# Attention by pairs of heads with one transpose bank and shared copies, and expert tokens transposed four experts at a time

## The chip, the cores and the metric

One core of a Trainium2 chip runs the whole program. The metric is device time in microseconds (us), the median of several executions. Beside it there is one profiled execution, from which all rows below come.

## The reference

One inference step of a two-layer backbone on 256 context tokens and 1024 latent tokens, width 1024, all in fp32. Layer 0 mixes by a long convolution and by attention (8 query heads of 64, 2 key heads); layer 1 by a gated linear recurrence. Each layer ends with 16 experts, each of which picks its own tokens: 32 of the context and 128 of the latents. What the change touches, cut to its core:

```python
def block_attention(q, k, v):                    # per head and block of 128 queries
    s = jnp.einsum('bqkgd,bskd->bkgqs', qblk, k) * scale
    p = jax.nn.softmax(s, axis=-1)
    return jnp.einsum('bkgqs,bskd->bqkgd', p, v)

def expert_choice_ffn(h, router_w, w_gu, w_down):
    aff = softmax(xf @ router_w); gate, idx = lax.top_k(aff.T, cap)
    xin = xf[idx]
    a, u = jnp.split(jnp.einsum('ecd,edf->ecf', xin, w_gu), 2, axis=-1)
    out = jnp.einsum('ecf,efd->ecd', jax.nn.silu(a) * u, w_down) * gate[..., None]
    return zeros.at[idx.reshape(-1)].add(out.reshape(-1, D))
```

Context queries see the 256 context keys (2 tiles of 128), latent queries the cached context and all latents (10 tiles).

## The kernel before

The program is a chain of stages, each a block of five instruction streams (PE, ACT, DVE, POOL, SP) that wait for one another by semaphores; a stream's order is its order in the code.

**Attention** (`attention`, line 900) goes through 80 items, each one head and one tile of 128 queries: 64 latent items with 10 key tiles and 16 context items with 2. Of an item, PE computes the scores (call them S, line 930: 512, 512 and 256 columns, contraction over the 64 rows of one head), DVE takes the row maximum (lines 996, 998), ACT the exponential with its row sum (972), DVE normalises (1000 to 1002), PE transposes the probabilities (T, line 957: 10 tiles of 128x128), ACT copies them from PSUM to SBUF (984) and PE multiplies by the values (P, line 941, 64 output rows); DVE copies the result out (1008). The scores have one buffer of three PSUM banks, the transposes four banks `t_ps`, the output one. PE's order is S of item i+1, T of item i, P of item i-1. The two heads of a pair stand in rows 0 to 63 and 64 to 127 of `qT` and `kT`, and their results in the same halves of `o_ps`.

**Experts** (`experts`, line 1283, once per layer, after `route`, line 1152): SP streams 12 MB of weights per expert in 12 pieces. POOL gathers the 128 latent and the 32 context rows of the next expert (lines 1338, 1339) and scatters the results. PE transposes the gathered rows (lines 1370, 1371) into one PSUM tile of 2x160 columns, in four groups of two latent and two context transposes each; ACT scales them into `xT` (1431). Then PE computes 16 chains of 8 matmuls on 160 columns (gate and up, line 1385), ACT and DVE form silu(a) times u (1439, 1461), and PE multiplies by the down weights, for latents (1398) and, as four column groups of 32, for context (1408). The groups of transposes for expert e+1 stand after the gate and up matmuls of e and between its four down chains. Experts 0 to 14 run as a hardware loop on every engine.

Of the kernel before, what the change touches and what calls it, by code (L numbers as in the profile page):

```python
# [899 lines left out]
def attention(nc, A, S, qT, kT, v, yT):  # L900


    items = [(2 * pr + r, t, 0 if t < CT else CT, CT if t < CT else KT - CT)
             for pr in range(4) for t in range(NT) for r in range(2)]
    N = len(items)
    chunks = [[(k, min(4, nk - k)) for k in range(0, nk, 4)] for _, _, _, nk in items]
    first = [sum(len(c) for c in chunks[:i]) for i in range(N + 1)]
    KMAX = KT - CT
    with ExitStack() as ctx:
        sb, ps, sem = scope(nc, ctx, "att")  # L910
        p = sb("p", [P, 2, KMAX * P])
        pT = sb("pT", [P, 2, KMAX, P])
        top, part = sb("top", [P, N, 3]), sb("part", [P, N, 3])
        nmax, total = sb("nmax", [P, N]), sb("total", [P, N])
# [3 lines left out]
        qk, maxed, exped, normed, v_steps, tr, tr_out, pv, o_out = (  # L918
            sem("qk"), sem("maxed"), sem("exped"), sem("normed"), sem("v"), sem("tr"), sem("tr_out"), sem("pv"), sem("o_out"))
        block = ctx.enter_context(nc.Block())  # L920

        @block.tensor
        def _(pe):
            def scores(i):
                h, t, k0, nk = items[i]
                r = h % 2
                for j, (k, n) in enumerate(chunks[i]):
                    if i >= 1:
                        pe.wait_ge(exped, min(first[i - 1] + j + 1, first[i]))
                    nc.tensor.matmul(s_ps[:, k * P:(k + n) * P], qT[64 * r:64 * r + HD, h // 2, t * P:(t + 1) * P],  # L930
                                     kT[64 * r:64 * r + HD, h // 4, (k0 + k) * P:(k0 + k + n) * P], start=True, stop=True).then_inc(qk, 1)

            def products(i):
                h, t, k0, nk = items[i]
                r = h % 2
                if i >= 2:
                    pe.wait_ge(o_out, i - 1)
                for j, (k, n) in enumerate(chunks[i]):
                    pe.wait_ge(tr_out, first[i] + j + 1)
                    for a in range(k, k + n):  # L940
                        m = nc.tensor.matmul(o_ps[64 * r:64 * r + HD, 0:P], v[:, k0 + a, (h // 4) * HD:(h // 4 + 1) * HD],  # L941
                                             pT[:, i % 2, a, :], start=(a == 0), stop=(a == nk - 1))
                m.then_inc(pv, 1)

            scores(0)
            for i in range(N):
                h, t, k0, nk = items[i]
                r = h % 2
                if i + 1 < N:
                    scores(i + 1)  # L950
                pe.wait_ge(normed, i + 1)
                for j, (k, n) in enumerate(chunks[i]):
                    c = first[i] + j
                    if c >= 4:
                        pe.wait_ge(tr_out, c - 3)
                    for a in range(n):
                        m = nc.tensor.transpose(t_ps[c % 4][:, a * P:(a + 1) * P], p[:, i % 2, (k + a) * P:(k + a + 1) * P],
                                                S["ident"][:, :])
                    m.then_inc(tr, 1)
                if i >= 1:  # L960
                    products(i - 1)
            products(N - 1)

        @block.scalar
        def _(act):
            def exps(i):
                h, t, k0, nk = items[i]
                act.wait_ge(maxed, i + 1)
                if i >= 2:
                    act.wait_ge(tr, first[i - 1])  # L970
                for j, (k, n) in enumerate(chunks[i]):
                    nc.scalar.activation(p[:, i % 2, k * P:(k + n) * P], s_ps[:, k * P:(k + n) * P], ACT.Exp, bias=nmax[:, i:i + 1],  # L972
                                         accum_out=part[:, i, j:j + 1]).then_inc(exped, 1)

            exps(0)
            for i in range(N):
                if i + 1 < N:
                    exps(i + 1)
                if i >= 2:
                    act.wait_ge(pv, i - 1)  # L980
                for j, (k, n) in enumerate(chunks[i]):
                    c = first[i] + j
                    act.wait_ge(tr, c + 1)
                    nc.scalar.activation(pT[:, i % 2, k:k + n, :].rearrange("p a c -> p (a c)"), t_ps[c % 4][:, 0:n * P],
                                         ACT.Copy).then_inc(tr_out, 1)

        @block.vector
        def _(dve):
            steps = Count(v_steps)

            def softmax(i):
                h, t, k0, nk = items[i]
                nch = len(chunks[i])
                for j, (k, n) in enumerate(chunks[i]):
                    dve.wait_ge(qk, first[i] + j + 1)
                    r = nc.vector.tensor_reduce(top[:, i, j:j + 1], s_ps[:, k * P:(k + n) * P], AX_X, ALU.max)
                steps.link(dve, r)
                nc.vector.tensor_reduce(nmax[:, i:i + 1], top[:, i, 0:nch], AX_X, ALU.max, negate=True).then_inc(maxed, 1)  # L998
                dve.wait_ge(exped, first[i + 1])
                steps.link(dve, nc.vector.reduce_sum(total[:, i:i + 1], part[:, i, 0:nch], AX_X))  # L1000
                steps.link(dve, nc.vector.reciprocal(total[:, i:i + 1], total[:, i:i + 1]))
                nc.vector.tensor_scalar(p[:, i % 2, 0:nk * P], p[:, i % 2, 0:nk * P], total[:, i:i + 1], None, ALU.mult).then_inc(normed, 1)

            def output(i):
                h, t, _, _ = items[i]
                r = h % 2
                dve.wait_ge(pv, i + 1)
                nc.vector.tensor_copy(yT[64 * r:64 * r + HD, h // 2, t * P:(t + 1) * P], o_ps[64 * r:64 * r + HD, 0:P]).then_inc(o_out, 1)

            softmax(0)  # L1010
            for i in range(N):
                if i + 1 < N:
                    softmax(i + 1)
                if i >= 1:
                    output(i - 1)
            output(N - 1)
# [124 lines left out]
def load_expert(sp, A, layer, w, w_in, j, e):  # L1141

    if j < 8:
        jj, part = divmod(j, 2)
        c0 = part * FH + jj * SW
        src = A["moe_w_gu"][layer][bass.ds(e, 1), :, c0:c0 + SW]
    else:
        src = A["moe_w_down"][layer][bass.ds(e, 1), :, (j - 8) * SW:(j - 7) * SW]
    sp.dma_start(w[:, j, :, :], src.rearrange("a (k p) n -> p (a k) n", p=P)).then_inc(w_in[j], 16)


def route(nc, A, S, tag, hnT, layer, idx, gates, expert_w, expert_w_in, next_modulation=False):
# [3 lines left out]
    with ExitStack() as ctx:  # L1156
# [12 lines left out]
        pt = ps("pt", [P, 4 * NE])  # L1169
# [21 lines left out]
        def _(pe):  # L1191
# [41 lines left out]
        def _(dve):  # L1233
# [37 lines left out]
            dve.wait_ge(tr2, 1)  # L1271
            for c in range(2):
# [10 lines left out]
def experts(nc, A, S, tag, layer, xn_dram, x_dram, idx, gates, w, w_in):  # L1283
# [6 lines left out]
    CC = CP + CL  # L1290
    with ExitStack() as ctx:
        sb, ps, sem = scope(nc, ctx, tag)
        xl, xc = sb("xl", [P, D]), sb("xc", [CP, D])
        xT = sb("xT", [P, KD, CC])
# [3 lines left out]
        icg, ics = [sb("icg0", [CP, 1], U32), sb("icg1", [P, 1], U32)], [sb("ics0", [CP, 1], U32), sb("ics1", [P, 1], U32)]  # L1298
        gate_f = sb("gate_f", [P, 2, D])
        pgu = [ps(f"pgu{i}", [P, CC]) for i in range(4)]  # L1300
        pxt = ps("pxt", [P, 2 * CC])
# [5 lines left out]
        gate_in, p_steps, o_free, issued = sem("gate_in"), sem("p_steps"), sem("o_free"), sem("issued")  # L1307
        block = ctx.enter_context(nc.Block())

        @block.sync  # L1310
        def _(sp):
# [7 lines left out]
            with sp.Fori(1, NE) as e:  # L1319
                for j in range(12):  # L1320
                    if j < 8 and j % 2 == 0:
                        sp.wait_ge(gu_mm, e * 16 + (4 * (j // 2) + 4 - 16))
# [889 lines left out]
```

## Time and profile before

| | us |
|---|---|
| median of 3 runs (4649.28 to 4650.81) | 4650.71 |
| the profiled execution | 4647.39 |
| its span, first to last instruction | 4645.6 |
| PE busy in the span | 4148.2 (89%) |
| DVE, ACT, POOL busy | 1825.1, 1245.0, 200.7 |
| mean granted TensorE clock | 0.945 of 2.4 GHz |

PE = TensorE matmul, PEld = its weight loads (which overlap), DVE = VectorE, ACT = ScalarE, POOL = GpSimd, SP = SyncE. Attention takes the stretch from 651 to 1078 us, the experts of layer 0 that from 1345 to about 2270, those of layer 1 that up to 4606. An fp32 matmul shows in the records as two passes. A matmul's recorded end is modelled, so the start of the next block is the better mark.

### The profile page before, as it was taken

Reading aid. Unit: us, or ns where it says so; the run is one execution under the profiler, and the core shown is the slowest. Engines: PE = TensorE matmul, PEld = TensorE weight load, DVE = VectorE, ACT = ScalarE, POOL = GpSimd, SP = SyncE. Lnnn points to the kernel's source line nnn. Section 1 sums busy time; section 2 is a strip of 40 time slices with the busy share of each in tenths; the row PEclk is TensorE's granted clock in tenths of the full one; section 3 lists DMA queues with packets and bytes.
Section 4 is the critical chain, followed back from the end, with each engine's and each line's share of the span. In section 5 each row is a group of like instructions: output and inputs, shape, how many; then the busy total and the mean of one; then the engine's idle time right before and its main releaser. Section 6 shows DMA issues by size and latency. Waiting matters only on the chain. (4 is left out here: it accounts for less than half of the span.)

```text
span 4645.6 us, 59698 instructions
## 1 busy us (share of the span) xinstructions
PE 4148.2 (89%) x23973; PEld 3289.7 (71%) x23973; DVE 1825.1 (39%) x3112; ACT 1245.0 (27%) x2593; POOL 200.7 (4%) x304
## 2 busy tenths in 40 slices
PE   5798999999759999999699999999768299999996
PEld 1454456665339999998588888888644199999995
DVE  4324355552351111111248888888832611111111
ACT  1211135552201111111244454444423011111111
POOL 0000000000000000001000000000000001000000
PEclk8899989999879999999799999999889599999998
DMA  6201100003487888777410101110032478888884
GB/s 224 86 14 58 35 1 1 1 1 118 174 273 244 252 249 248 239 239 239 123 29 26 31 16 31 31 31 17 7 137 95 129 224 252 251 252 251 251 249 160
DMA packets 522238, 614.81 MB, mean 132 GB/s; under 512 B 16460, under 2 KB 466632, under 8 KB 521449
## 3 DMA queue, kind: packets, MB, share of 16 engines
q1 hardware_dynamic: 502216, 543.33, 36.0%
q0 software_dynamic: 16832, 58.73, 5.0%
q10 hardware_dynamic: 3040, 10.68, 0.6%
q8 instruction: 102, 1.67, 0.1%
q14 instruction: 48, 0.39, 0.0%
HBM read 558.86 MB, written 53.84 MB: 132 GB/s over the span
## 5 line engine op out<-in xcount | busy, mean ns | idle before, releaser
L1385 PEld LDWEIGHTS moe_pgu<-moe_xT,mw_w 128*128 128x128 f32 x8192 | 1118.7, 191 | 15.6 <-issue 15.6
L1385 PE MATMUL moe_pgu<-moe_xT,mw_w 128*128 128x160 f32 x8192 | 1126.4, 300 | 3.0 <-ACT moe_xT L1431 3.0
L1461 DVE TENSOR_TENSOR moe_hT<-moe_sg,moe_pgu 128x160 f32<-128x160 f32 x256 | 82.3, 322 | 1028.0 <-PE moe_pgu L1385 944.9
L1398 PE MATMUL moe_pol<-mw_w,moe_hT 128*128 128x256 f32 x2048 | 474.6, 385 | 0.8 <-DVE moe_hT L1461 0.8
L1642 PE MATMUL rec_pz<-step_hnT,rec_w 128*128 128x256 f32 x1920 | 425.1, 380 | 10.8 <-DMA rec_w<-in_r_w_in 8.8
L1398 PEld LDWEIGHTS moe_pol<-mw_w,moe_hT 128*128 128x128 f32 x2048 | 379.0, 190 | 52.8 <-DVE moe_hT L1461 1.3
L1642 PEld LDWEIGHTS rec_pz<-step_hnT,rec_w 128*128 128x128 f32 x1920 | 362.8, 191 | 59.7 <-DMA rec_w<-in_r_w_in 9.1
L1439 ACT ACTIVATE moe_sg<-moe_pgu 128x160 f32<-128x160 f32 x256 | 77.8, 304 | 1124.9 <-PE moe_pgu L1385 1124.9
L1431 ACT ACTIVATE moe_xT<-moe_pxt,step_modcol 128x128 f32<-128x128 f32 (+1 forms) x512 | 172.5, 417 | 534.2 <-PE moe_pxt L1371 534.2
L1646 PE MATMUL rec_pz<-rec_w,step_hnT 128*128 128x256 f32 x1280 | 284.8, 381 | 15.2 <-ACT rec_zg L1717 15.2
L1646 PEld LDWEIGHTS rec_pz<-rec_w,step_hnT 128*128 128x128 f32 x1280 | 241.5, 191 | 49.8 <-ACT rec_zg L1717 18.0
L1465 DVE SCALAR_TENSOR_TENSOR moe_ol<-moe_pol,step_gates,moe_gate_f 128x512 f32<-128x512 f32 x64 | 48.1, 751 | 518.6 <-PE moe_pol L1398 518.6
L1672 PE MATMUL rec_pg<-rec_ring 128*128 128x128 f32 x1600 | 198.3, 283 | 49.9 <-DVE rec_AT L1958 18.6
L1672 PEld LDWEIGHTS rec_pg<-rec_ring 128*128 128x128 f32 x1600 | 194.6, 198 | 55.6 <-DVE rec_ring L1937 20.3
L383 PE MATMUL hin_psm<-step_hnT,hin_w 128*128 128x512 f32 (+1 forms) x576 | 209.1, 526 | 10.6 <-DMA hin_w<-in_e_w_in 10.6
L383 PEld LDWEIGHTS hin_psm<-step_hnT,hin_w 128*128 128x128 f32 x576 | 110.7, 193 | 106.3 <-issue 89.9
L930 PE MATMUL att_s_ps<-l0p_kT,l0p_qT 64*128 64x512 f32 (+1 forms) x416 | 172.2, 545 | 10.4 <-ACT att_p L972 8.6
L972 ACT ACTIVATE att_p<-att_s_ps,att_nmax 128x512 f32<-128x512 f32 (+1 forms) x208 | 123.7, 602 | 205.7 <-DVE att_nmax L998 205.7
L941 PE MATMUL att_o_ps<-att_pT,l0p_v 128*64 128x128 f32 x1344 | 165.6, 278 | 0.0
L1085 PE MATMUL op_psm<-op_w,l1o_yr 128*128 128x512 f32 x320 | 142.8, 603 | 19.2 <-DMA l1o_yr<-scratch_yr 19.2
L941 PEld LDWEIGHTS att_o_ps<-att_pT,l0p_v 128*64 128x64 f32 x1344 | 145.9, 138 | 14.0 <-issue 13.4
L1770 ACT ACTIVATE rec_ring<-rec_ring 128x1280 f32<-128x1280 f32 x112 | 138.5, 1264 | 37.2 <-DVE rec_ring L1914 32.3
(316 smaller groups left out, 4648.7 us busy)
## 6 DMA issues: line engine op xcount, KB each, us to landing
mw_w<-in_moe_w_gu SPq DMA_DIRECT2D x256, 1024.0 KB, 10.1
mw_w<-in_moe_w_down SPq DMA_DIRECT2D x128, 1024.0 KB, 10.2
mod_w_ring<-in_mod_w SPq DMA_DIRECT2D x24, 1024.0 KB, 14.4
mw_w<-in_mod_w SPq DMA_DIRECT2D x24, 1024.0 KB, 14.3
rec_w<-in_r_w_in SPq DMA_DIRECT2D x40, 512.0 KB, 3.9
scratch_xm<-op_x ACTq DMA_DIRECT2D x20, 512.0 KB, 2.6
scratch_xn<-op_xn POOLq DMA_DIRECT2D x20, 512.0 KB, 5.1
hin_w<-in_e_w_in SPq DMA_DIRECT2D x12, 512.0 KB, 6.7
```

The costliest lines, as they stand in the source:

```text
L383: m = nc.tensor.matmul(psm[j % NPS][:, 0:n * P], w[:, i % 2, k, part, :], hnT[:, k, t0 * P:(t0 + n) * P], start=(k == 0), stop=(k == KD - 1))
L930: nc.tensor.matmul(s_ps[:, k * P:(k + n) * P], qT[64 * r:64 * r + HD, h // 2, t * P:(t + 1) * P], kT[64 * r:64 * r + HD, h // 4, (k0 + k) ...
L941: m = nc.tensor.matmul(o_ps[64 * r:64 * r + HD, 0:P], v[:, k0 + a, (h // 4) * HD:(h // 4 + 1) * HD], pT[:, i % 2, a, :], start=(a == 0), s ...
L972: nc.scalar.activation(p[:, i % 2, k * P:(k + n) * P], s_ps[:, k * P:(k + n) * P], ACT.Exp, bias=nmax[:, i:i + 1], accum_out=part[:, i, j: ...
L1085: m = nc.tensor.matmul(psm[t % NB][:, h * 512:(h + 1) * 512], lhs(k)[:, t * P:(t + 1) * P], w[:, k, h * 512:(h + 1) * 512], start=(k == 0) ...
L1385: m = nc.tensor.matmul(pgu[2 * (f % 2) + part][:, :], w[:, j, k, (f % 2) * P:(f % 2 + 1) * P], xT[:, k, :], start=(k == 0), stop=(k == KD ...
L1398: m = nc.tensor.matmul(pol[q // 2][:, (q % 2) * SW:(q % 2 + 1) * SW], hT[:, k, 0:CL], w[:, 8 + q, k, :], start=(k == 0), stop=(k == KD - 1))
L1431: r = nc.scalar.activation(xT[:, k, c0:c0 + n], pxt[:, j * CC + c0:j * CC + c0 + n], ACT.Identity, bias=mc[:, layer, 3, c, k:k + 1], scale ...
L1642: m = nc.tensor.matmul(pz[i % 3][:, 0:2 * P], w[:, k, n // NZU, :], hnT[:, k, c0:c0 + 2 * P], start=(k == 0), stop=(k == KD - 1))
L1646: m = nc.tensor.matmul(pz[i % 3][:, 0:2 * RD], hnT[:, k, t * P:(t + 1) * P], w[:, k, 3:5, :].rearrange("p a c -> p (a c)"), start=(k == 0) ...
L1672: into_banks(h, (d, i), lambda o, t: nc.tensor.matmul(o, kb[:, t * P:(t + 1) * P], qb[:, t * P:(t + 1) * P], start=True, stop=True))
L1770: nc.scalar.activation(r, r, ACT.Exp).then_inc(exped, 1)
```

## The change

Attention: an item is now a pair of heads, 40 pairs in all, the 8 context pairs first. The scores have two buffers of three banks, one per head; S alternates between the two heads' row halves, P between their output halves. The probabilities are transposed in groups of four tiles into one single bank; ACT copies groups 0, 1, 2 and 4 of a latent pair and DVE group 3. Maximum and exponential take up to 1024 and 1280 columns in one instruction. PE's order is T group 0, S of the next pair, then T groups 1 to 4 with a slice of the P of the pair before after each.

Experts: the context rows of four experts are gathered and transposed together (128 rows), into a ring in `hnT`; a context turn stands after experts 3, 7 and 11. A turn is two groups of four 128x128 transposes. `route` gains four small matmuls and a copy that form the index `idx_four`. The hardware loops are unrolled, POOL's index copies are gone, and the scatter's wait stands before the next scatter.

```diff
-    items = [(2 * pr + r, t, 0 if t < CT else CT, CT if t < CT else KT - CT)
-             for pr in range(4) for t in range(NT) for r in range(2)]
+    pairs = [(pr, t, 0, CT) for pr in range(4) for t in range(CT)] + [(pr, t, CT, KT - CT) for pr in range(4) for t in range(CT, NT)]
+    groups = [[tl[g:g + 4] for g in range(0, len(tl), 4)] for tl in tiles]
+    by_dve = [g == 3 for gr in groups for g in range(len(gr))]
...
-        s_ps = ps("s_ps", [P, 3 * 512])
-        t_ps = [ps(f"t_ps{i}", [P, 512]) for i in range(4)]
+        s_ps = ps("s_ps", [P, 2, 3 * 512])
+        t_ps = ps("t_ps", [P, 512])
...
+            def scores(i, j):
+                for r in range(2):
+                    if i:
+                        pe.wait_ge(exped, 2 * (i - 1) + r + 1)
+                    nc.tensor.matmul(s_ps[:, r, k * P:(k + n) * P], qT[64 * r:64 * r + HD, pr, t * P:(t + 1) * P],
...
+            def transposes(i, g):
+                pe.wait_ge(normed, 2 * i + 1 + max(r for r, _ in group))
+                copied(pe, gfirst[i] + g)
...
+            def products(i, a0, a1):
+                if a0 == 0:
+                    copied(pe, gfirst[i + 1])
+                    if i:
+                        pe.wait_ge(o_out, i)
+                for a in range(a0, a1):
+                    for r in range(2):
...
+                for g in range(ng):
+                    transposes(i, g)
+                    if g == 0 and i + 1 < N:
+                        for j in range(len(chunks[i + 1])):
+                            scores(i + 1, j)
+                    if i and (g or ng == 1):
...
+                for g in range(3):
+                    copy(i, g)
+                if i + 1 < N:
+                    exp(i + 1, 0)
+                copy(i, 4)
+                if i + 1 < N:
+                    exp(i + 1, 1)
...
+                if i + 1 < N:
+                    maxes(i + 1)
+                copy(i, 3)
+                if i + 1 < N:
+                    normalise(i + 1, 0)
+                if i + 1 < N:
+                    normalise(i + 1, 1)
+                if i:
+                    output(i - 1)
...
+            for j in range(4):
+                m = nc.tensor.matmul(pt[32 * j:32 * j + CAP[0], 4 * NE:], topf[:, 0, 0:CAP[0]], S["ident"][0:NE, j:NE:4],
+                                     start=True, stop=True, tile_position=(0, 32 * j))
...
+        turns = [("c", 0), ("l", 0)]
+        for e in range(1, NE):
+            turns += [("l", e)] + ([("c", e // 4)] if e % 4 == 0 else [])
...
+                for j in range(4):
+                    m = nc.tensor.transpose(pxt[:, j * P:(j + 1) * P], src[:, (4 * g + j) * P:(4 * g + j + 1) * P], S["ident"][:, :])
...
+                moves = [(turn, g) for turn in coming(e) for g in range(2)]
+                if moves:
+                    transposes(*moves[0])
+                pe.wait_ge(multiplied, NF * (e + 1))
...
+                    if q + 1 < len(moves):
+                        transposes(*moves[q + 1])
```

PE in the middle of attention before, one latent item: S (L930) of the next item, T (L957) of this one into three of the four banks `att_t_ps0` to `att_t_ps3`, P (L941) of the one before.

```order
L930 MATMUL att_s_ps<-l0p_kT,l0p_qT 128x512 x2
L930 MATMUL att_s_ps<-l0p_kT,l0p_qT 128x256
L957 MATMUL att_t_ps3<-step_ident,att_p 128x128 x4
L957 MATMUL att_t_ps0<-step_ident,att_p 128x128 x4
L957 MATMUL att_t_ps1<-step_ident,att_p 128x128 x2
L941 MATMUL att_o_ps<-att_pT,l0p_v 64x128 x10
```

PE at the same place now, one latent pair (S is L942, T is L951, P is L962), from S to the group of transposes that begins the next pair:

```order
L942 MATMUL att_s_ps<-l0p_kT,l0p_qT 128x512 x4
L942 MATMUL att_s_ps<-l0p_kT,l0p_qT 128x256 x2
L951 MATMUL att_t_ps<-step_ident,att_p 128x128 x4
L962 MATMUL att_o_ps<-att_pT,l0p_v 64x128 x4
L951 MATMUL att_t_ps<-step_ident,att_p 128x128 x4
L962 MATMUL att_o_ps<-att_pT,l0p_v 64x128 x6
L951 MATMUL att_t_ps<-step_ident,att_p 128x128 x4
L962 MATMUL att_o_ps<-att_pT,l0p_v 64x128 x4
L951 MATMUL att_t_ps<-step_ident,att_p 128x128 x4
L962 MATMUL att_o_ps<-att_pT,l0p_v 64x128 x6
L951 MATMUL att_t_ps<-step_ident,att_p 128x128 x4
```

Two heads share one S block and one P block cut in four, and every group of T goes into the same bank.

ACT in the middle of attention before: the three exponentials (L972) of the next item, then the three copies (L984) of this one.

```order
L972 ACTIVATE att_p,att_part<-att_s_ps,att_nmax 128x512 x2
L972 ACTIVATE att_p,att_part<-att_s_ps,att_nmax 128x256
L984 ACTIVATE att_pT<-att_t_ps3 128x512
L984 ACTIVATE att_pT<-att_t_ps0 128x512
L984 ACTIVATE att_pT<-att_t_ps1 128x256
```

ACT there now: the second head's exponential (L991) of one pair, copies of groups 0 to 2 (L999), the next pair's first exponential, the copy of group 4, and its second exponential.

```order
L991 ACTIVATE att_p,att_total<-att_s_ps,att_nmax 128x1280
L999 ACTIVATE att_pT<-att_t_ps 128x512 x3
L991 ACTIVATE att_p,att_total<-att_s_ps,att_nmax 128x1280
L999 ACTIVATE att_pT<-att_t_ps 128x512
L991 ACTIVATE att_p,att_total<-att_s_ps,att_nmax 128x1280
```

The second exponential stands behind the copy of the last group, and the next pair's first copy behind that exponential.

PE at the end of the gate and up matmuls of an expert before (`moe_xl` are latent rows, `moe_xc` context rows; the rows without a tile are the loop's registers and waits):

```order
L1385 MATMUL moe_pgu<-moe_xT,mw_w 128x160 x16
L1389 REGISTER_ALU
L1370 MATMUL moe_pxt<-step_ident,moe_xl 128x128
L1371 MATMUL moe_pxt<-step_ident,moe_xc 128x32
L1370 MATMUL moe_pxt<-step_ident,moe_xl 128x128
L1371 MATMUL moe_pxt<-step_ident,moe_xc 128x32
L1392 REGISTER_ALU
L1396 ISA
L1398 MATMUL moe_pol<-mw_w,moe_hT 128x256 x8
L1403 REGISTER_ALU
L1370 MATMUL moe_pxt<-step_ident,moe_xl 128x128
L1371 MATMUL moe_pxt<-step_ident,moe_xc 128x32
```

PE there now, a whole expert without a context turn:

```order
L1455 MATMUL moe_pgu<-step_hnT,mw_w 128x160 x128
L1438 MATMUL moe_pxt<-step_ident,moe_xl 128x128 x4
L1467 MATMUL moe_pol<-mw_w,moe_hT 128x256 x8
L1438 MATMUL moe_pxt<-step_ident,moe_xl 128x128 x4
L1467 MATMUL moe_pol<-mw_w,moe_hT 128x256 x24
L1477 MATMUL moe_poc<-mw_w,moe_hT 32x256 x32
```

Two groups of four stand where four groups of four stood; after experts 3, 7 and 11 there are four.

## Rows read from the trace of the kernel before

**Rows 1.** Waits in attention, 650 to 1075: engine, line, releaser: us, times, longest

```profile
ACT att_p L972 <- DVE att_nmax L998: 205.7, 80, 5.4
```

**Rows 2.** Timeline of PE in attention: start, us, engine, line, operation

```profile
804.94 2.41 PE L930 MATMUL att_s_ps<-l0p_kT,l0p_qT 64*128 64x512 f32 x6
807.28 1.31 PE L957 MATMUL att_t_ps<-step_ident,att_p 128*128 128x128 f32 x10
808.52 2.40 PE L941 MATMUL att_o_ps<-att_pT,l0p_v 128*64 128x128 f32 x20
810.85 2.41 PE L930 MATMUL att_s_ps<-l0p_kT,l0p_qT 64*128 64x512 f32 x6
```

**Rows 3.** Groups by line and shape in attention: busy us, mean ns | idle before

```profile
L996 DVE TENSOR_REDUCE att_top<-att_s_ps 128x1 f32<-128x512 f32 x128 | 87.6, 690 | 29.3 <-PE att_s_ps L930 28.8
L972 ACT ACTIVATE att_p<-att_s_ps,att_nmax 128x512 f32<-128x512 f32 x128 | 86.9, 683 | 178.5 <-DVE att_nmax L998 178.5
L984 ACT ACTIVATE att_pT<-att_t_ps 128x512 f32<-128x512 f32 x128 | 69.7, 606 | 0.9 <-PE att_t_ps L957 0.9
L1002 DVE TENSOR_SCALAR att_p<-att_p,att_total 128x1280 f32<-128x1280 f32 x64 | 56.7, 886 | 2.2
L972 ACT ACTIVATE att_p<-att_s_ps,att_nmax 128x256 f32<-128x256 f32 x80 | 37.8, 473 | 27.2 <-DVE att_nmax L998 27.2
L996 DVE TENSOR_REDUCE att_top<-att_s_ps 128x1 f32<-128x256 f32 x80 | 33.3, 416 | 8.7 <-PE att_s_ps L930 8.6
```

**Rows 4.** Timeline of the expert stage, PE, one whole expert

```profile
1422.27 35.04 PE L1385 MATMUL moe_pgu<-moe_xT,mw_w 128*128 128x160 f32 x256
1457.15 0.27 PE L1370 MATMUL moe_pxt<-step_ident,moe_xl 128*128 128x128 f32 x1
...
1457.96 3.72 PE L1398 MATMUL moe_pol<-mw_w,moe_hT 128*128 128x256 f32 x16
...
1474.71 3.66 PE L1408 MATMUL moe_poc<-mw_w,moe_hT 128*32 128x256 f32 x64
1478.30 5.97 PE L1385 MATMUL moe_pgu<-moe_xT,mw_w 128*128 128x160 f32 x42
```

**Rows 5.** Timeline of the last item of attention, all engines

```profile
1072.09 1.31 PE L957 MATMUL att_t_ps<-step_ident,att_p 128*128 128x128 f32 x10 [0.55 <-DVE att_p L1002]
1072.85 1.36 ACT L984 ACTIVATE att_pT<-att_t_ps 128x512 f32<-128x512 f32 x3 [0.87 <-PE att_t_ps L957]
...
1073.34 4.20 PE L941 MATMUL att_o_ps<-att_pT,l0p_v 128*64 128x128 f32 x40
...
1077.57 0.29 DVE L1008 COPY l_filt<-att_o_ps 64x128 f32<-64x128 f32 x1 [1.52 <-PE att_o_ps L941]
```

**Rows 6.** Timeline of the first context items of attention

```profile
651.01 1.19 PE L930 MATMUL att_s_ps<-l0p_kT,l0p_qT 64*128 64x256 f32 x2 [1.76 <-PEq L80]
...
653.26 0.19 ACT L972 ACTIVATION_READ_ACCUMULATOR att_p<-att_s_ps,att_nmax 128x1 f32 x1
```

**Rows 7.** Windows: us, busy by engine, granted clock, DMA share, GB/s

```profile
651.00:661.00 10.00, 8.00 (x20) 3.95 (x21) 4.52 (x18) 3.76 (x10) 0.00 (x0) 0.50 0.00 1
771.00:781.00 10.00, 8.41 (x36) 4.43 (x35) 5.57 (x16) 4.40 (x14) 0.00 (x0) 1.00 0.00 0
1480.20:1538.60 58.40, 58.40 (x419) 53.10 (x419) 6.27 (x15) 9.40 (x26) 6.78 (x9) 1.00 0.81 248
```

**Rows 8.** Timeline of the last expert of layer 0, which has no transposes

```profile
2241.72 0.32 DVE L1461 TENSOR_TENSOR moe_hT<-moe_sg,moe_pgu 128x160 f32<-128x160 f32 x1 [4.03 <-PE moe_pgu L1385]
2242.10 13.68 PEld L1398 LDWEIGHTS moe_pol<-mw_w,moe_hT 128*128 128x128 f32 x64 [0.65 <-DVE moe_hT L1461]
```

**Rows 9.** Timeline of the start of the expert stage of layer 0

```profile
1352.25 0.47 PE L1370 MATMUL moe_pxt<-step_ident,moe_xl 128*128 128x128 f32 x1 [8.58 <-DMA moe_xl<-scratch_xn,moe_icg]
...
1363.52 8.69 PE L1385 MATMUL moe_pgu<-moe_xT,mw_w 128*128 128x160 f32 x42 [1.51 <-ACT moe_xT L1431]
```

**Rows 10.** DMA queues of the page: packets, MB, share of 16 engines

```profile
q8 instruction: 102, 1.67, 0.1%
```

More of the change, by code:

```diff
@@ L922, in _ @@
         @block.tensor
         def _(pe):
[L924 to L943, printed above, removed]
@@ L964, in _, with exp @@
+            products(N - 1, 0, pairs[N - 1][3])
         @block.scalar
         def _(act):
-            def exps(i):
-                h, t, k0, nk = items[i]
-                act.wait_ge(maxed, i + 1)
+            def exp(i, r):
+                nk = pairs[i][3]
                 if i >= 2:
[L970 to L973, printed above, removed]
@@ L975, in _, with copy @@
-            exps(0)
+                    act.wait_ge(tr, gfirst[i - 1])
+                act.wait_ge(maxed, 2 * i + r + 1)
+                nc.scalar.activation(p[:, i % 2, r, 0:nk * P], s_ps[:, r, 0:nk * P], ACT.Exp, bias=nmax[:, 2 * i + r:2 * i + r + 1],
+                                     accum_out=total[:, 2 * i + r:2 * i + r + 1]).then_inc(exped, 1)
+            def copy(i, g):
+                if g >= len(groups[i]):
+                    return
+                group = groups[i][g]
+                act.wait_ge(tr, gfirst[i] + g + 1)
+                nc.scalar.activation(pT[:, i % 2, 4 * g:4 * g + len(group), :].rearrange("p a c -> p (a c)"),
+                                     t_ps[:, 0:len(group) * P], ACT.Copy).then_inc(act_out, 1)
@@ new lines, in normalise, with copy @@
+            def normalise(i, r):
+                nk, x = pairs[i][3], 2 * i + r
+                dve.wait_ge(exped, x + 1)
+                steps.link(dve, nc.vector.reciprocal(total[:, x:x + 1], total[:, x:x + 1]))
+                nc.vector.tensor_scalar(p[:, i % 2, r, 0:nk * P], p[:, i % 2, r, 0:nk * P], total[:, x:x + 1], None, ALU.mult).then_inc(normed, 1)
+            def copy(i, g):
+                if g >= len(groups[i]):
+                    return
+                if i >= 2:
+                    dve.wait_ge(pv, i - 1)
+                dve.wait_ge(tr, gfirst[i] + g + 1)
+                nc.vector.tensor_copy(pT[:, i % 2, 4 * g:4 * g + 4, :].rearrange("p a c -> p (a c)"), t_ps[:, :]).then_inc(dve_out, 1)
@@ L1354, in scatter @@
-                pool.wait_ge(c_added, e * 16 + 16)
-                pool.sem_inc(o_free, 1)
-            pool.sem_inc(o_free, 1)
-            gather(0, first=True)
-            with pool.Fori(0, NE - 1) as e:
-                gather(e + 1)
+            gather_c(0)
+            gather_l(0)
+            for e in range(NE):
+                if e + 1 < NE:
+                    gather_l(e + 1)
+                if e % 4 == 0 and e + 4 < NE:
+                    gather_c(e // 4 + 1)
                 scatter(e)
-            scatter(NE - 1)
+            pool.wait_ge(l_added, 16 * NE)
@@ L1376, in expert @@
+            for turn in turns[0:2]:
+                for g in range(2):
+                    transposes(turn, g)
+            for e in range(NE):
+                for f in range(NF):
                     for part in range(2):
@@ L1410, in expert @@
                 m.then_inc(oc_mm, 1)
-            pe.wait_ge(xl_in, 16)
-            pe.wait_ge(xc_in, 16)
-            for g in range(4):
-                if g:
-                    pe.wait_ge(xT_out, g)
-                transposes(0, g)
-            with pe.Fori(0, NE - 1) as e:
-                expert(e, False)
-            expert(NE - 1, True)
         mc = S["modcol"]
@@ L1447, in _, with to_xT @@
-            with act.Fori(0, NE - 1) as e:
-                expert(e, False)
-            expert(NE - 1, True)
+            def to_xT(turn, g):
+                kind, n = turn
+                act.wait_ge(tr, after(kind, n) - 1 + g)
+                for j in range(4):
+                    k = 4 * g + j
+                    src = pxt[:, j * P:(j + 1) * P]
+                    if kind == "l":
+                        c, dst = 1, ring[:, k, n % 8, 0:CL]
+                    else:
+                        c, dst, src = 0, ring[:, k, 4 * (n % 2):4 * (n % 2) + 4, CL:CC], src.rearrange("p (s c) -> p s c", c=CP)
+                    r = nc.scalar.activation(dst, src, ACT.Identity, bias=mc[:, layer, 3, c, k:k + 1], scale=mc[:, layer, 4, c, k:k + 1])
+                r.then_inc(xT_out, 1)
```

275 lines of the change are left out of this document (137 added, 138 removed).

## The prediction

> **What bounds the kernel now.** I read the page's shares first (PE 89%), then windows by stage, then the waits and timelines of the two stages that change. In attention ACT waits 205.7 us for DVE's maxima [rows 1], yet that costs nothing: PE goes from S to T to P to S without a hole, 2.34, 1.24 and 2.33 us from start to start, 5.91 per latent item [rows 2]. So the 64 latent items are 378 of attention's 426.9 us (first S 651.01, last copy out to 1077.86 [rows 5, 6]); context items, the cold start and the tail are the other 49. Look for the sum of PE's three blocks to equal the period: no other engine sets it. The expert stage reads the same way: PE is busy 58.40 of 58.40 us at DMA share 0.81 [rows 7], one expert takes 56.03 us (1422.27 to 1478.30) [rows 4]. There, only PE work taken away counts.
>
> **Attention: PE's work.** A pair has the instructions of two items, and the same 20 transposes. What changes is who stands beside whom. S of two heads sits in different row halves, P in different output halves, now adjacent in the queue. For output groups the trace shows the effect: the context down matmuls, four groups of 32, go through 64 passes of 256 columns in 3.66 us (0.057 each), where full-width passes of the same 256 columns take 3.72 for 16 (0.23) [rows 4]: four run at once. So P of a pair, 40 passes at 0.105 (4.20 for 40 [rows 5]), is 4.2 if alone and 2.1 if two run at once; I take 2.3. For row halves no row shows anything, as S of two heads is never adjacent before. Bounds for S of a pair: 2.34 (wholly beside each other) and 4.68 (one after the other; not more, the passes are the same; not less, two halves are all there is). The nearest row is that of the output groups, so I take 2.34. PE's work per pair is then about 2.34 + 2.5 + 2.3 = 7.1 instead of 11.82.
>
> The Trainium skill, TensorE: Matmul & The Clock Gate, section "Measured speedup vs the span model", gives four row tiles a speedup of 3.07 instead of 4. No run here shows it yet. By that efficiency of 0.77 (an estimate) S of a pair would be 3.04, and the total below 22 us higher.
>
> **Attention: the chain that comes in its place.** All five groups of T go through one bank, so each waits until the copy before has left it, and ACT does the second exponential after the copy of group 4, while S of the next pair needs that exponential. Piece by piece, from T group 4 on:
> - T start to copy start: 0.76 (1072.09 to 1072.85 [rows 5]).
> - copy of 512 columns, to the next ACT instruction: 1.36 us for 1280 columns [rows 5], so 0.54.
> - exponential of 1280 columns: 683 at 512, 473 at 256 [rows 3], so 0.82 ns a column, 1.31; the row-sum read adds 0.19 [rows 6]: 1.50.
> - semaphore to PE: 0.06 (2241.72 + 0.32 to 2242.10 [rows 8]).
> - S of the next pair, 2.34, with T group 1 queued behind it.
> - groups 1, 2 and 3 to the next group: 0.76 + a whole copy 0.606 [rows 3] + 0.06 = 1.43 each, 4.29.
>
> Sum: 9.49 per pair. The slices of P (0.5 to 0.7 each) lie in the 0.85 that each copy takes, and T group 0 beside the exponential, so they add nothing; if P's halves don't run together, slices of 0.84 and 1.26 stick out by some 0.8 a pair. A normalise must be done before T group 2; it takes 1.05 (0.886 [rows 3] and a reciprocal) right after the exponential, some 5 us early. DVE's own work is 2 x (1.24 for 1024 columns + 0.42 + 0.16) + 2 x 1.05 + 0.6 + 0.29 = 6.6, from 690 and 416 ns [rows 3]. Its copy of group 3 stands behind all maxima of the next pair, which end some 5.6 after S starts (3.64 of work from 2.0, when the first 1024 columns are out); group 3 is there at 2.34 + 2 x 1.43 + 0.76 = 5.96. So DVE has only 0.4 to spare: it is what is late next.
>
> The Trainium skill, TensorEngine Tiling (Array Packing), "Tiling Modes", key properties, says that a change of tiling mode drains the engine, which speaks against this order: a latent pair now changes mode ten times instead of six. The rows agree that a change costs something: P takes 2.33 from start to start for 20 passes of 0.105 [rows 2, 5], so about 0.23. If all four more were on the path, 32 pairs would lose 29 us; I count none, since T waits there for a copy anyway.
>
> Attention after: the 8 context pairs run at 0.50 clock like the first items [rows 7]; one head takes 2.44 from S to the end of the exponential (651.01 to 653.45 [rows 6]), the second adds 0.5, normalise 0.65, four cold transposes 1.0: 4.6 a pair, 37. Then 31 latent periods of 9.49, 294; the first at the slow clock, +5; the last pair has no S, but its T group 1 waits for a copy behind the last exponential: T 1 at 9.85, T 4 at 14.1, copy 15.5, 40 passes of P and the copy out, 18.5. Sum 355: **-72**.
>
> **Experts.** Four groups of transposes took 0.81 each (1457.15 to 1457.96 [rows 4]). A new group is four 128x128 transposes without the 32-row ones between, 0.124 each (1.24 for ten [rows 2]) with a fill, 0.55. The first group also covers DVE's last product: in an expert without transposes PE waits until 0.06 after it [rows 8], which is 0.58 after the first transpose would start, so it can't shrink below 0.58. Saved: 4 x 0.81 - 0.58 - 0.55 = 2.11, in experts with a context turn 1.01. Twelve and three per layer: 28.4, both layers **-57**. ACT's four scalings of 128 columns lie beside a down chain of 3.6, and a 54 us period asks for little more than the DMA share of 0.81 [rows 7]; a tighter stream would show as PE waiting for `mw_w`.
>
> At each layer's start, from the first gathered row to the first matmul took 11.27 (1352.25 to 1363.52 [rows 9]). Four groups remain, slightly shorter without 32-row work (-0.5); POOL no longer copies an index (-1.2, estimated from two copies and their wait), and the first transposes need only the context rows. `route` gains four tiny matmuls and a copy before the barrier (+0.5). But 512 KB of context rows come where 128 KB came, which costs between nothing and 2. I take -1.5 a layer, **-3**. The end of the kernel is unchanged.
>
> **Sum.** -72 - 57 - 3 = -132 from the profiled execution's 4647.4: 4515. The median of the runs is 3.3 above that execution: **4518**.
>
> **The rivals.**
> 1. *S of the two heads doesn't overlap.* For it: no row shows row halves at once. Against: output groups do. The period is 9.49 + 2.34 = 11.83, as long as two items before; 32 x 2.34 = +75: 4593.
> 2. *The handshakes through one bank are dearer.* Ten changes of mode and waits on two semaphores each; 0.3 more on five handshakes is 1.5 a pair, +48: 4566. Against it: the 0.76 of rows 5 already contains one such edge.
> 3. *Unrolled code.* Instruction queue q8 moved 1.67 MB in 102 packets [rows 10], while some 12,000 of PE's pairs of instructions came out of a loop. Straight-line code adds about as much again, some 100 packets, in the stage where DMA is at 0.81. If PE waits 0.6 us for each, the experts' gain is gone: 4578. Against it: 256 instructions per packet last over 10 us of matmuls.
> 4. *Slower than before: the clock.* PE is busy to about three quarters in the new attention, with a hole of 0.8 at each exponential. If the granted clock stays at 0.50 there, as at 651 to 661 [rows 7], S, T and P of a pair take twice 7.1 and PE binds again at 14.5: 32 x 5 = +160: 4678. It beats the whole gain only if it holds in over four fifths of the pairs. Against it: 84% busy at 771 to 781 ran at 1.00 [rows 7], and when PE is slow it is also always busy, which brought the clock back before.
>
> **How the numbers follow.** Forecast with S beside S, 4500 to 4545 by itself: 0.66. Rival 1: 0.13. Rival 2: 0.09. Rival 3: 0.06. Rival 4: 0.04. Everything a little better than the sum, 4495: 0.02. A range from 4498 to 4592 leaves out rival 4, half of rival 1 and the tails of the forecast, some 0.15. A measurement of this kernel can tell 0.2%, 9 us, from no change. All cases but rival 4 are faster by more; of its 0.04 I leave 0.01 for a clock that comes and goes and ends level. Faster 0.96, same 0.01, slower 0.03.
>
> **What would show it.** In attention: S of a pair from its start to the next T in about 2.4 us (rival 1: 4.7); T groups 1.43 apart after S (rival 2: more); DVE's copy of group 3 waiting for T and not the reverse; a latent period of 9.5 us; granted clock 1.00 past the context pairs, which are at 0.50 (rival 4). PE's share falls there to about 75%, and its idle time is put down to ACT's copies and exponentials. In the experts: period 53.9 us, 55.0 after experts 3, 7 and 11, PE still without idle time; waits of PE on nothing visible that come back every 128 matmuls would be rival 3. The prediction is wrong if attention takes more than 400 us, or if the expert period stays above 55.

## The result and the profile after

The changed kernel took **4491.9 us** (median of 4 runs, 4490.6 to 4493.6), the kernel before 4650.0 beside it: ratio 0.966, 95% interval 0.9644 to 0.9677. The forecast was 4518; the time lies 6 us below the range. The profiled execution is 157 us shorter. By markers in the two traces (first S, last copy out, first and last expert matmuls, next load), attention gave 79.3 us (predicted 72), the experts' bodies 34.8 + 34.9 = 69.7 (57), the starts of the two expert stages, from the last transposes of `route` to the first gate and up matmul, 3.7 (3), their ends 3.1 (0), the rest 1.3 (0).

One latent pair on PE, which answers to [rows 2] (columns as there; `x12` of S are two heads):

```profile
802.65 3.08 PE L942 MATMUL att_s_ps<-l0p_kT,l0p_qT 64*128 64x512 f32 x12
805.67 0.66 PE L951 MATMUL att_t_ps<-step_ident,att_p 128*128 128x128 f32 x4
806.25 0.66 PE L962 MATMUL att_o_ps<-att_pT,l0p_v 128*64 128x128 f32 x8
807.06 0.63 PE L951 MATMUL att_t_ps<-step_ident,att_p 128*128 128x128 f32 x4
807.62 0.88 PE L962 MATMUL att_o_ps<-att_pT,l0p_v 128*64 128x128 f32 x12
808.42 0.66 PE L951 MATMUL att_t_ps<-step_ident,att_p 128*128 128x128 f32 x4
...
810.02 0.63 PE L951 MATMUL att_t_ps<-step_ident,att_p 128*128 128x128 f32 x4 [0.35 <-DVE att_pT L1046]
...
811.98 3.08 PE L942 MATMUL att_s_ps<-l0p_kT,l0p_qT 64*128 64x512 f32 x12
814.99 0.66 PE L951 MATMUL att_t_ps<-step_ident,att_p 128*128 128x128 f32 x4
```

From S to S is 9.33 us. Groups of T start 1.39, 1.36 and 1.60 apart. PE now has holes behind P's slices of 8 passes: the first of them ends at 806.91 and the next T starts at 807.06, and before the T at 810.02 PE stands still for 0.35. Behind the slice of 12 (1.36) there is none: there T and P need as long as the bank does. ScalarE in the same pair, with what ended its wait:

```profile
810.69 0.60 ACT L999 ACTIVATE att_pT<-att_t_ps 128x512 f32<-128x512 f32 x1 [1.06 <-PE att_t_ps L951]
811.18 1.32 ACT L991 ACTIVATE att_p<-att_s_ps,att_nmax 128x1280 f32<-128x1280 f32 x1
812.39 0.20 ACT L991 ACTIVATION_READ_ACCUMULATOR att_p<-att_s_ps,att_nmax 128x1 f32 x1
```

And VectorE's copy of the fourth group:

```profile
809.19 0.69 DVE L1046 COPY att_pT<-att_t_ps 128x512 f32<-128x512 f32 x1 [1.12 <-PE att_t_ps L951]
```

Of the 205.7 us for which ScalarE waited for maxima [rows 1] 12.5 are left, all of them before 700 us; it waits for T, and so does VectorE's copy. Read down from T at 810.02: copy at 810.69, exponential at 811.18, its sum out at 812.59, T 2.40 later at 814.99.

An expert on PE, without a context turn, against [rows 4]:

```profile
1339.37 35.04 PE L1455 MATMUL moe_pgu<-step_hnT,mw_w 128*128 128x160 f32 x256
1374.24 0.60 PE L1438 MATMUL moe_pxt<-step_ident,moe_xl 128*128 128x128 f32 x4
1374.89 3.72 PE L1467 MATMUL moe_pol<-mw_w,moe_hT 128*128 128x256 f32 x16
1378.45 0.60 PE L1438 MATMUL moe_pxt<-step_ident,moe_xl 128*128 128x128 f32 x4
1378.88 10.53 PE L1467 MATMUL moe_pol<-mw_w,moe_hT 128*128 128x256 f32 x48
1389.34 3.66 PE L1477 MATMUL moe_poc<-mw_w,moe_hT 128*32 128x256 f32 x64
1392.93 35.04 PE L1455 MATMUL moe_pgu<-step_hnT,mw_w 128*128 128x160 f32 x256
```

The period is 53.56 (1339.37 to 1392.93) where it was 56.03; with a context turn it is 54.44. Windows, as [rows 7] (granted clock, DMA share and GB/s stand last):

```profile
701.00:711.00 10.00, 7.50 (x39) 4.51 (x39) 5.70 (x12) 4.89 (x8) 0.00 (x0) 0.84 0.01 2
800.00:900.00 100.00, 94.62 (x772) 65.27 (x766) 67.08 (x130) 52.06 (x87) 0.00 (x0) 1.00 0.00 1
1400.00:1480.00 80.00, 79.95 (x588) 76.12 (x588) 7.91 (x20) 7.37 (x23) 3.89 (x3) 1.00 0.92 290
```

The instruction queue, as [rows 10]:

```profile
q8 instruction: 189, 3.10, 0.3%
```

The clock is 0.84 in the second ten microseconds of the latent pairs (0.66 in the first, 0.99 in the third) and 1.00 from then on, and PE stays busy in the experts at DMA share 0.92 with 87 more instruction packets.

### The profile page after: what moved, and what is told of

Read it like the earlier page. It is cut to its first block and busy times, and to the rows that moved or that the text cites. A ratio compares the mean times of both kernels' runs of the same rounds, so it can differ in the third digit from the quotient of the medians.

```text
span 4488.5 us, 55794 instructions
## 1 busy us (share of the span) xinstructions
PE 3975.2 (89%) x23797; PEld 3179.5 (71%) x23797; DVE 1803.6 (40%) x2946; ACT 1111.2 (25%) x2045; POOL 156.6 (3%) x152
## 5 line engine op out<-in xcount | busy, mean ns | idle before, releaser
L1455 PEld LDWEIGHTS moe_pgu<-step_hnT,mw_w 128*128 128x128 f32 x8192 | 1117.6, 191 | 16.5 <-issue 16.5
L1455 PE MATMUL moe_pgu<-step_hnT,mw_w 128*128 128x160 f32 x8192 | 1125.2, 300 | 3.4 <-ACT step_hnT L1495 3.4
L1467 PE MATMUL moe_pol<-mw_w,moe_hT 128*128 128x256 f32 x2048 | 457.6, 381 | 2.3 <-DVE moe_hT L1519 1.0
L1495 ACT ACTIVATE step_hnT<-moe_pxt,step_modcol 128x128 f32<-128x128 f32 x320 | 120.3, 456 | 357.1 <-PE moe_pxt L1438 357.1
L951 PE MATMUL att_t_ps<-step_ident,att_p 128*128 128x128 f32 x672 | 112.6, 292 | 34.1 <-DVE att_p L1038 14.7
L2013 DVE COPY_PREDICATED rec_AT<-rec_maskb,rec_pg 128x512 f32<-128x512 uint8 (+1 forms) x192 | 109.9, 625 | 48.6 <-PE rec_pg L1727 47.2
L1135 PEld LDWEIGHTS op_psm<-op_w,l1o_yr 128*128 128x128 f32 x320 | 60.7, 193 | 94.1 <-issue 94.1
L951 PEld LDWEIGHTS att_t_ps<-step_ident,att_p 128*128 128x128 f32 x672 | 73.2, 145 | 73.4 <-issue 54.0
```

The source lines that it names most:

```text
L951: m = nc.tensor.transpose(t_ps[:, n * P:(n + 1) * P], p[:, i % 2, r, a * P:(a + 1) * P], S["ident"][:, :])
L1135: m = nc.tensor.matmul(psm[t % NB][:, h * 512:(h + 1) * 512], lhs(k)[:, t * P:(t + 1) * P], w[:, k, h * 512:(h + 1) * 512], start=(k == 0) ...
L1455: m = nc.tensor.matmul(pgu[2 * (f % 2) + part][:, :], w[:, j, k, (f % 2) * P:(f % 2 + 1) * P], ring[:, k, e % 8, :], start=(k == 0), stop= ...
L1467: m = nc.tensor.matmul(pol[q // 2][:, (q % 2) * SW:(q % 2 + 1) * SW], hT[:, k, 0:CL], w[:, 8 + q, k, :], start=(k == 0), stop=(k == KD - 1))
L1495: r = nc.scalar.activation(dst, src, ACT.Identity, bias=mc[:, layer, 3, c, k:k + 1], scale=mc[:, layer, 4, c, k:k + 1])
L2013: last = nc.vector.copy_predicated(at, maskb[:, j:j + 1, :].broadcast_to([P, nt, P]), src)
```

## The experiments

Medians are of 4 to 11 runs; the kernel before took 4647.5 to 4648.3 beside them.

**Each half alone.** The edit: the old `attention` function, or the old `route` and `experts`, in the other kernel.

```diff
-def attention(...)   # before's        -def route, experts(...)   # before's
+def attention(...)   # after's         +def route, experts(...)   # after's
```

> The changed attention alone; route and experts are as before. Theory (the two halves of the change add up, each in its own stage): the markers of the two traces put the attention 79.3 us earlier, so 4650 - 79 = 4571 us, with experts at a period of 56.03 us as before. Rival (the attention took over part of what the experts gave, for instance by a different start of the route or the weights' arrival): a gain under 74 or over 84 us.

> The changed route and experts alone; the attention is as before. Theory (the halves add up): 157.1 - 79.3 = 78 us go, 4572 us; the experts' periods are 53.6 us, and 54.4 us with a context turn, as in the changed kernel, and the attention's PE period stays 5.91 us per item. Rival (the two halves help each other): the two gains of this run and the attention's alone add up to less than 150 us.

Measured: 4566.6 (ratio 0.9824, 0.9807 to 0.984) and 4570.8 (0.9835, 0.9818 to 0.9851): 81.7 and 77.5 us less, 159 in all. The halves add up.

**Do S's two heads run beside each other?** First by another order:

```diff
-for j in chunks: for r in range(2): scores(i + 1, j, r)
+for r in range(2): for j in chunks: scores(i + 1, j, r)
```

> In the changed kernel the scores of a pair are issued all of head 0 first and then all of head 1, in place of chunk by chunk with the heads in turn. Theory (matmuls on the two halves of the rows run beside each other when they follow each other directly, and S of two heads takes 2.40 us from its release, about what one head took before): without it S takes 2 x 2.34 = 4.7 us, less the 0.6 us by which head 0's may start before the second exp is done: T's second group of a pair comes 1.7 to 2.3 us later, and the kernel 53 to 74 us: 4545 to 4566 us. Rival (they don't run beside each other, S is short because the chunks are): within 5 us of the changed kernel.

Measured: 4502.0 (4493.0 to 4505.6), +10. Neither expectation. S with the T before and behind it, and T of the next pair:

```profile
809.34 0.66 PE L951 MATMUL att_t_ps<-step_ident,att_p 128*128 128x128 f32 x4
809.93 3.38 PE L942 MATMUL att_s_ps<-l0p_kT,l0p_qT 64*128 64x512 f32 x12
813.24 0.66 PE L951 MATMUL att_t_ps<-step_ident,att_p 128*128 128x128 f32 x4
...
818.96 0.66 PE L951 MATMUL att_t_ps<-step_ident,att_p 128*128 128x128 f32 x4
```

S takes 3.31 from start to T instead of 3.01, so 0.3 x 32 = 10 us; one of the four runs shows almost nothing of it, so this rests on the period (9.62 against 9.33) more than on the time. Either the heads overlapped even so, or they never did. Then with a wait that forbids it:

```diff
+if r and j == 0: pe.wait_ge(qk, 2 * first[i] + len(chunks[i]))   # head 0 done
```

> As the run with the scores issued head by head (4502 us, S 3.38 us from its start to the next group), with one wait more: head 1's scores start only when head 0's are done. Theory (that run was hardly slower because the second head's matmuls ran beside the first's though they stood behind all of them; two row halves do work at once): S takes 2.34 + 0.1 + 2.34 = 4.8 us from its start, 1.4 us more than without the wait, 32 x 1.4 = 45 us: 4540 to 4555 us. Rival (the halves hardly overlap, and S of two heads is short for another reason): within 5 us of 4502 us.

Measured: 4565.0, +63. PE in the same place:

```profile
807.93 0.66 PE L953 MATMUL att_t_ps<-step_ident,att_p 128*128 128x128 f32 x4
808.51 4.88 PE L944 MATMUL att_s_ps<-l0p_kT,l0p_qT 64*128 64x512 f32 x12
813.33 0.66 PE L953 MATMUL att_t_ps<-step_ident,att_p 128*128 128x128 f32 x4
...
819.05 0.66 PE L953 MATMUL att_t_ps<-step_ident,att_p 128*128 128x128 f32 x4
```

4.82 from start to T, as expected, and a pair takes 11.12 instead of 9.62: 1.50 x 32 = 48 us. The overlap is shown. The other 15 us were not foreseen. 7.6 of them are lost by the first maxima of a latent pair (697.4 against 689.8), in the context pairs at half clock; the rest fits the clock of the next windows (not shown by a run of its own), 0.50 here and in the ten microseconds behind it, where the run before had 0.73 and 1.00:

```profile
711.00:721.00 10.00, 8.12 (x22) 3.94 (x22) 3.00 (x8) 2.50 (x4) 0.00 (x0) 0.50 0.00 0
```

**And P's?** The same change of order within a slice:

```diff
-for a in range(a0, a1): for r in range(2): matmul(o_ps[64 * r ...], pT[r * nk + a])
+for r in range(2): for a in range(a0, a1): matmul(o_ps[64 * r ...], pT[r * nk + a])
```

> In the changed kernel each slice of P is issued all tiles of head 0 first and then those of head 1, in place of tile by tile with the heads in turn. Theory (products of two heads, on two halves of the columns, run beside each other: 0.56 us for x8 where 0.105 us a pass as before would make 0.84; the slices lie just within the turn-round of a transposed group): x8 costs 0.84 and x12 1.26 us, the gaps between the groups grow by 0.0 and 0.5 us, and the kernel by 20 to 40 us: 4512 to 4532 us. Rival (the slices have room in the turn-round of the groups whatever they cost): within 5 us of the changed kernel.

Measured: 4500.2, +8.3, between the two. PE around one slice:

```profile
810.12 0.63 PE L951 MATMUL att_t_ps<-step_ident,att_p 128*128 128x128 f32 x4
810.68 1.15 PE L962 MATMUL att_o_ps<-att_pT,l0p_v 128*64 128x128 f32 x12
811.75 0.66 PE L951 MATMUL att_t_ps<-step_ident,att_p 128*128 128x128 f32 x4
```

`x12` holds PE 1.07 instead of 0.80 and T's gap is 1.63 instead of 1.36. Two slices a pair are so, but the one behind the fifth group stands beside the exponential: 0.27 x 32 = 8.6 us. In turn, 12 passes take 0.80, where 0.105 each [rows 5] would make 1.26: the output halves overlap too.

**Is it the chain through ScalarE?** In the changed kernel:

```diff
-copy(i, 4); exp(i + 1, 1)
+exp(i + 1, 1); copy(i, 4)
```

> In the changed kernel ScalarE does the second exp of the next pair before the fifth copy, in place of after it. Theory (the latent pair's period of 9.32 us is a chain: the fifth group of transposes, its copy on ScalarE, the second exp and its read of the sum, S, and the groups after it; the copy's 0.5 us is in it for the order on ScalarE alone): about 0.5 us of 9.3 goes per latent pair, 32 x 0.5 = 15 us: 4477 us. Rival (the fifth copy is what the next pair's first group waits for, since all groups share one bank; the copy then comes later and the period stays or grows): 4490 us or more, up to 4491 + 32 x 0.9 = 4520 us.

Measured: **4476.5** (0.9628, 0.9615 to 0.9641), the 15 us expected. ScalarE:

```profile
802.60 0.60 ACT L999 ACTIVATE att_pT<-att_t_ps 128x512 f32<-128x512 f32 x1 [0.77 <-PE att_t_ps L951]
803.09 1.32 ACT L991 ACTIVATE att_p<-att_s_ps,att_nmax 128x1280 f32<-128x1280 f32 x1
...
804.40 1.33 ACT L991 ACTIVATE att_p<-att_s_ps,att_nmax 128x1280 f32<-128x1280 f32 x1
...
805.70 0.60 ACT L999 ACTIVATE att_pT<-att_t_ps 128x512 f32<-128x512 f32 x1
```

Copy, two exponentials and the copy at 805.70 follow one another without a pause, and T (806.40) waits for that copy. PE behind it:

```profile
806.96 2.42 PE L942 MATMUL att_s_ps<-l0p_kT,l0p_qT 64*128 64x512 f32 x12
809.31 0.66 PE L951 MATMUL att_t_ps<-step_ident,att_p 128*128 128x128 f32 x4
```

The next S starts at 815.73: the pair is 8.77, bound by the one bank and ScalarE's order.

**Two banks for T.** From that kernel; to make room, S of both heads lies in five banks, which also changes the order of its chunks and of the maxima, and S now waits for both exponentials (not shown):

```diff
-t_ps = ps("t_ps", [P, 512])
+t_ps = [ps(f"t_ps{x}", [P, 512]) for x in range(2)]
-copied(pe, gfirst[i] + g)
+copied(pe, max(0, gfirst[i] + g - 1))
```

> The kernel with the second exp ahead of the fifth copy (the run before of 4476.5 us, latent pair's period 8.77 us), and the transposed probabilities in two banks in turn, so that a group of transposes waits for the copy of the group before the last; the scores of two heads share five banks for that, the maxima of the two 256-column parts are taken before the first head's is whole (0.4 us later than now). Theory (the groups' gaps of 1.37 to 1.60 us are the turn-round of the one bank, and TensorE would need some 0.57 + 0.57 or 0.80 us of each, with S 2.4 us some 8.0 us a pair): the period falls to 8.0 to 8.4 us, 12 to 25 us in all: 4452 to 4465 us. Rival (it is the loop from S over the maxima, the first exp and the first normalisation to the next pair's first group that sets 8.77 us; with the maxima later it grows): 8.8 to 9.2 us a pair, 4477 to 4490 us.

Measured: **4449.9** (0.9575, 0.9562 to 0.9588), 42 us under the changed kernel and 2 below what was expected. PE from the third group of T in one pair to that in the next:

```profile
801.62 0.66 PE L954 MATMUL att_t_ps<-step_ident,att_p 128*128 128x128 f32 x4
...
804.80 2.42 PE L945 MATMUL att_s_ps<-l0p_kT,l0p_qT 64*128 64x256 f32 x12
807.15 0.66 PE L954 MATMUL att_t_ps<-step_ident,att_p 128*128 128x128 f32 x4
807.74 0.66 PE L965 MATMUL att_o_ps<-att_pT,l0p_v 128*64 128x128 f32 x8
808.33 0.66 PE L954 MATMUL att_t_ps<-step_ident,att_p 128*128 128x128 f32 x4
808.91 0.88 PE L965 MATMUL att_o_ps<-att_pT,l0p_v 128*64 128x128 f32 x12
809.72 0.66 PE L954 MATMUL att_t_ps<-step_ident,att_p 128*128 128x128 f32 x4
```

And a window of this run:

```profile
800.00:900.00 100.00, 100.00 (x899) 67.31 (x895) 76.56 (x151) 61.01 (x101) 0.00 (x0) 1.00 0.01 1
```

8.10 a pair, and PE is busy for 100 of 100 us: it is the bound again. With the first exponential also moved ahead:

```diff
-copy(i, 2); exp(i + 1, 0)
+exp(i + 1, 0); copy(i, 2)
```

> As the run with two banks, and the first exp of the next pair ahead of the third copy on ScalarE, in place of after it. By the theory (the banks' turn-round bounds the pair) the third copy comes 1.3 us later, two banks give the groups that much room only in part: within 5 us of the run with two banks, or up to 15 us over it. By the rival (the loop over maxima, first exp and normalisation bounds it) the first exp comes up to 1 us sooner per pair: 10 to 32 us under the run with two banks.

Measured: 4464.5, 15 us more, as the theory had it. ScalarE now stands in front of the third copy, waiting for maxima:

```profile
806.56 1.33 ACT L992 ACTIVATE att_p<-att_s_ps,att_nmax 128x1280 f32<-128x1280 f32 x1 [0.98 <-DVE att_nmax L1038]
```

**Do the loops cost anything?** In the kernel before:

```diff
-with pe.Fori(0, NE - 1) as e:      # and so on SP, POOL, ACT, DVE
+for e in range(0, NE - 1):
```

> The kernel before with the experts' loops written out on every engine, and nothing else changed. Theory (the loops cost nothing within an expert, since TensorE runs without pause there, and only the end of the loops and what GpSimd does around them show): the periods stay 56.0 us, the time from the last context matmuls to the next stage's first load falls by up to 1.5 us a layer: 4646 to 4650 us. Rival (the loop's branches sit between experts on TensorE): 0.1 to 0.5 us of each period goes, 3 to 16 us in all: 4634 to 4647 us, with periods below 55.9 us.

Measured: 4645.4 (0.9996, 0.9987 to 1.0005): no difference. The period is 56.03. From the last context matmuls to the next load (layer 0) it takes 16.6 us against 16.75 before and 15.2 after, so the loops are not what made the ends shorter.

**What made the old groups dear?** In the kernel before, the 32 context rows lie in a tile of 128 (the others zero); four groups at four places stay:

```diff
-nc.tensor.transpose(pxt[... CC], xc[0:CP, ...], S["ident"][0:CP, 0:CP])
+nc.tensor.transpose(pxt[... 128], xc[:, ...], S["ident"][:, :])
```

> The kernel before, with the context rows transposed as a full 128 x 128 tile (32 rows gathered, the rest zero, 32 of the columns read out), so that all transposes have one shape; their number and places are as before. Four groups a pass cost 56.03 - 53.06 = 2.97 us per expert before; two of 128 rows cost 0.44 after. Theory (the change of shape between 128 and 32 rows, four times a group, is what made the old groups dear): a group then costs about 0.44 behind the first, the period is 53.1 + 3 x 0.45 = 54.4 us, and the kernel 30 x 1.6 = 48 us faster: about 4602 us. Rival (it is the number of places at which the chain of matmuls is broken, and the read-outs that a group waits for): the period stays 56.0 us or a little over, 4645 to 4655 us.

Measured: 4600.6 (0.9898, 0.9882 to 0.9913). PE around the second group, and the next expert's start:

```profile
1421.27 35.04 PE L1388 MATMUL moe_pgu<-moe_xT,mw_w 128*128 128x160 f32 x256
...
1460.35 0.27 PE L1373 MATMUL moe_pxt<-step_ident,moe_xl 128*128 128x128 f32 x1
...
1460.79 3.62 PE L1401 MATMUL moe_pol<-mw_w,moe_hT 128*128 128x256 f32 x16
1464.24 0.27 PE L1373 MATMUL moe_pxt<-step_ident,moe_xl 128*128 128x128 f32 x1
...
1475.71 6.52 PE L1388 MATMUL moe_pgu<-moe_xT,mw_w 128*128 128x160 f32 x46
```

The period is 54.44. With more columns to move, a group takes 0.44 instead of 0.81, and the down chain behind it 3.45 instead of 3.56. The second group before started here, so that it was 4.37 from group to group [rows 4] and the down chain between them 3.56:

```profile
1461.52 0.27 PE L1370 MATMUL moe_pxt<-step_ident,moe_xl 128*128 128x128 f32 x1
```

The 32-row shape was the price: 1.59 us of the 2.47 that an expert gives.

## Why the prediction was right and where it failed

**The mechanism held.** PE's work for a pair fell from 11.82 to below the period, and the chain through the one bank took its place, as listed: T to copy 0.67 (0.76 predicted), copy 0.49 (0.54), exponential and read 1.41 (1.50), to the next T 2.40 (0.06 + 2.34), three groups 4.35 (4.29). Sum 9.32 against 9.49: 5.3 us over 31 pairs, most of the 7 by which attention was better. Moving one link confirms the chain.

**PE's own work was set too low, and it was luck that this cost nothing.** The prediction added 7.1 us a pair and looked for PE at about 75%; it is busy for 94.6 of 100 us. With two banks, where PE never waits, a pair takes 8.10: S 2.35, five groups of T at 0.59 (2.5 predicted for all), slices of P at 0.59 and 0.81, two of each (2.3 predicted). From 8 to 12 passes a slice grows by 0.22, so a pass costs 0.055, half of the 0.105 that it took before, and 0.15 belong to the slice itself. The changed kernel had 1.2 us of slack on PE where the prediction counted 2.4.

**S, rival 1.** From the second exponential's sum to the next T is 2.40, and with both heads free at once S takes 2.35 (806.96 to 809.31 in the run with the exponential first); one head alone took 2.34, two in series 4.82. The halves overlap almost wholly. The Trainium skill, TensorE: Matmul & The Clock Gate, "Measured speedup vs the span model", gives four row tiles 3.07 of 4. For two halves these rows give 2 x 2.34 / 2.35 = 1.99, and the prediction's estimate of 3.04 us from that page doesn't hold here.

**Rivals 2 to 4.** The handshakes were no dearer (T's gaps 1.39 and 1.36 against 1.43; only the fourth group, copied by VectorE, takes 1.60). 87 more packets stopped nothing. The clock rose to 1.00 within the first three latent pairs. That was not as safe as the prediction's row made it look: right behind the 84% at 771 to 781 [rows 7] the kernel before had 0.83 for ten microseconds.

**The step that failed** is "4 x 0.81 - 0.58 - 0.55 = 2.11, in experts with a context turn 1.01". Measured: 2.47 and 1.59, so 12 x 0.36 + 3 x 0.58 = 6.1 a layer, 12 us in all: the largest share of the 25 us that the sum missed. The step counted only the groups' own spans. The chains of `pol` behind the old groups took 1474.71 - 1457.96 - 3 x 0.81 = 14.3 us [rows 4], the new ones 1389.34 - 1374.89 - 0.43 = 14.0: 0.3 of the 0.36. And each further new group costs 0.44, not 0.55, which the context turns pay three times. The number stood in the trace before, in its last expert, which has no transposes:

```profile
2206.65 35.04 PE L1385 MATMUL moe_pgu<-moe_xT,mw_w 128*128 128x160 f32 x256
...
2256.11 3.66 PE L1408 MATMUL moe_poc<-mw_w,moe_hT 128*32 128x256 f32 x64
```

With 3.59 for the context matmuls [rows 4] it took 53.05, so the four groups cost 2.98 of the 56.03, where the sum of their spans has 4 x 0.81 - 0.58 = 2.66. The Trainium skill, TensorEngine Tiling (Array Packing), "Tiling Modes", says that a change of mode drains the engine. The prediction held that rule against the attention, where the 29 us that it allowed for did not come, and not for the experts, where it cost most: behind the first group, 0.48 us per group (from group to group 4.37 before, 3.89 without 32-row passes) over four changes, 0.12 each, and the 0.23 for two in the old P [rows 2, 5] says the same. That the shape is the price is shown by the run with full rows; that it is the changes, and not the 32-row transposes themselves, is not.

**Smaller terms.** The ends, set to 0, gave 1.5 and 1.6. It is not the loops, and not the experts alone either: behind layer 0 it takes 15.4 to the next load with the attention alone changed and 15.3 with `route` and `experts` alone. What it is stays open. Another 2.1 went between that load and the recurrence, but this may be one execution of the kernel before: 41.2 there, 37.9 to 39.8 in every other run, the two with the old attention and the old order of the experts among them. The starts gave 3.7 instead of 3. All five misses have one sign, and the forecast gave "everything a little better" a chance of 0.02: the lower end stood too near the sum.

## What to carry to other kernels

Price work that is taken out by a stretch of the same loop that runs without it, not by its own spans: what it does to its neighbours is in the first alone. When two streams overlap and PE stops being the bound, write out the chain link by link, and look in it for an instruction that stands there only by its engine's order; moving one such copy gave 15 us, a second bank, with the scores packed to make room for it, 27 more. On the same engine a few transposes of another shape can cost more than more transposes of the shape around them.

## What the runs showed of the hardware beyond that

- Matmuls of the second row half overlap with the first half's even when all of those stand ahead of them: 3.31 us for S in that order, 3.01 in turn (both with some 0.6 us in which only the first head may run), 4.82 if the second waits. In that order the records have a 64x256 matmul of the first head start at 811.7, behind six passes of 64x512, of which only four are its own head's.
- The granted clock (1.00 is 2.4 GHz, 0.50 is 1.2) rose later the less the two heads' S overlapped, with the same matmuls. In 691 to 701, 701 to 711 and 711 to 721 it was 0.66, 0.84 and 0.99 in the changed kernel, 0.50, 0.50 and 0.73 with S by head, and 0.50 throughout with S in series. PE was busy for 6.5, 7.5 and 9.5 of each 10 us in the first, 9.1, 8.0 and 9.5 in the second, 9.2, 9.0 and 8.1 in the third. Why is not shown.
